# A recurrence with the backward heads' halves exchanged and the inverse transposed on TensorE, and two low-rank columns of the input projection made one

## The reference

```python
def rwkv_prep(u, shift_w, decay_b0, decay_up, iclr_b0, iclr_up, k_k, k_a, g_up):
    u = dwconv(u, shift_w).astype(jnp.float32)
    r, k, v, w_lo, a_lo, g_lo = jnp.split(u, [RWKV_W, 2 * RWKV_W, o1, o2, o3], axis=-1)
    kk = to_heads(k * k_k)
    kk = kk / jnp.maximum(jnp.sqrt(jnp.sum(kk * kk, axis=-1, keepdims=True)), 1e-12)
    for d in range(2):
        decay = jnp.exp(-DECAY_SCALE * jax.nn.sigmoid(decay_b0[d] + jnp.tanh(w_lo) @ decay_up[d]))
        a = jax.nn.sigmoid(iclr_b0[d] + a_lo @ iclr_up[d])
        k_d = k * (1.0 + (a - 1.0) * k_a)
...
def wkv_scan(r, k, v, decay, kk, a, s0, reverse, emit):
    def step(s, inp):
        r_t, k_t, v_t, w_t, kk_t, b_t = inp
        sa = -jnp.einsum("bhvk,bhk->bhv", s, kk_t)
        s = (s * w_t[:, :, None, :] + sa[..., None] * b_t[:, :, None, :]
             + v_t[..., None] * k_t[:, :, None, :])
        y = jnp.einsum("bhvk,bhk->bhv", s, r_t) if emit else None
        return s, y
```

## Time and profile before

| | us |
|---|---|
| median of 3 runs | 4267.63 |
| their range | 4267.39 to 4275.46 |
| the profiled execution | 4272.21 |
| its span | 4270.2 |
| PE busy in the span | 3939.6 |
| DVE busy | 2489.1 |
| ACT busy | 1605.8 |

### The profile page before, as it was taken

One profiled execution on the slowest core, in us unless ns is written; L12 is line 12 of the kernel. 1 busy time (PEld: TensorE's weight loads), 2 busy tenths in 40 slices (PEclk: granted clock), 3 DMA queues, 4 the chain that ended last, 5 costly groups with the idle time before them and its releaser, 6 DMA issues.

```text
span 4270.2 us, 85377 instructions
## 1 busy us (share of the span) xinstructions
PE 3939.6 (92%) x37243; PEld 3037.8 (71%) x37243; DVE 2489.1 (58%) x3146; ACT 1605.8 (38%) x1948; POOL 103.8 (2%) x96
## 2 busy tenths in 40 slices
PE   7987988999999897898999979888899999999996
PEld 5866885588887676887488668544677777777774
DVE  5966774322231675775443334563677777777774
ACT  3244332200021345333100242552566565656563
POOL 0000000000000000000000000000000000000000
PEclk9989999999999998999999989998899999999998
DMA  5430001121112441001222221402899999999995
GB/s 222 169 126 3 4 4 62 42 69 60 60 67 78 162 167 60 5 4 43 79 90 98 92 105 50 148 1 75 304 346 345 352 348 349 341 347 350 353 349 176
DMA packets 114120, 651.82 MB, mean 153 GB/s; under 512 B 15008, under 2 KB 15008, under 8 KB 55968
## 3 DMA queue, kind: packets, MB, share of 16 engines
q1 hardware_dynamic: 101344, 610.74, 38.3%
q0 software_dynamic: 12464, 36.38, 3.1%
HBM read 637.55 MB, written 27.46 MB: 156 GB/s over the span
## 4 chain that ended last, share of the span: by engine, by line
PE 83%; DVE 9%; ACT 4%; issue 2%; DMA 2%; SPq 0%; DVEq 0%; POOL 0%; POOLq 0%; ACTq 0%
PE psum L852 54%; PE psum L1603 16%; PE psum L1629 5%; PE psum L1620 4%; PE psum L1596 1%; DVE work L2020 1%; DVE xt L1988 1%; DVE work L2343 1%; PE psum L1587 1%; PE psum L1577 1%; DMA ring<-w_in 1%; PE psum L1456 1%; ACT work L2775 0%; DMA ring<-stream 0%; ACT work L3020 0%
## 5 line engine op out<-in xcount | busy, mean ns | idle before, releaser
L852 PE MATMUL psum<-ht_parts,ahead_parts 128*128 128x512 f32 (+3 forms) x2064 | 699.6, 355 | 2.9 <-DVE ht_parts L1752 2.2
L852 PE MATMUL psum<-work 64*64 64x64 f32 (+2 forms) x12950 | 548.4, 238 | 78.2 <-ACT work L2775 26.4
L852 PEld LDWEIGHTS psum<-work 64*64 64x64 f32 (+1 forms) x12950 | 441.4, 138 | 150.3 <-issue 70.8
L852 PE MATMUL psum<-work_parts,ring_parts 128*128 128x512 f32 (+1 forms) x1504 | 540.9, 360 | 0.0
L852 PE MATMUL psum<-work_parts,ahead_parts 128*128 128x512 f32 (+1 forms) x1408 | 495.3, 363 | 17.7 <-ACT work_parts L2629 15.6
L852 PEld LDWEIGHTS psum<-ht_parts,ahead_parts 128*128 128x128 f32 (+2 forms) x2064 | 379.2, 186 | 68.7 <-DVE ht_parts L1752 3.7
L852 PEld LDWEIGHTS psum<-work_parts,ring_parts 128*128 128x128 f32 x1504 | 286.3, 190 | 46.7 <-issue 1.7
L852 PEld LDWEIGHTS psum<-work_parts,ahead_parts 128*128 128x128 f32 x1408 | 266.3, 190 | 63.3 <-issue 21.8
L1603 PE MATMUL psum<-work_parts 128*128 128x512 f32 x1024 | 273.7, 394 | 0.7 <-DVE ring_parts L2468 0.5
L2468 DVE TENSOR_TENSOR ring_parts<-ring,work_parts 128x2048 fp32r<-128x2048 f32 x97 | 221.9, 2288 | 75.9 <-ACT work_parts L3094 75.9
L852 PE MATMUL psum<-xt_parts,ahead_parts 128*128 128x512 f32 (+5 forms) x656 | 233.2, 356 | 17.7 <-ACT xt_parts L2629 12.0
(11 more groups left out here) (351 smaller groups left out, 6780.2 us busy)
## 6 DMA issues: line engine op xcount, KB each, us to landing
ring<-stream SPq DMA_DIRECT2D x192, 1024.0 KB, 5.0
ring<-w_in SPq DMA_DIRECT2D x192, 1024.0 KB, 6.7
ht<-w_in SPq DMA_DIRECT2D x64, 1024.0 KB, 5.9
ht<-w_out SPq DMA_DIRECT2D x64, 1024.0 KB, 7.4
ring<-w_out SPq DMA_DIRECT2D x64, 1024.0 KB, 7.0
xt<-x_wide SPq DMA_DIRECT2D x8, 391.5 KB, 15.2
xt<-x_wide POOLq DMA_DIRECT2D x1, 3132.0 KB, 10.9
xt_rows<-xt POOLq DMA_DIRECT2D x8, 391.5 KB, 2.7
```

The costliest lines, as they stand in the source:

```text
L852: mm = pe.matmul(*args, **kwargs)
```

## The change

In the recurrence the tiles of direction 1 are held with their halves exchanged where that lets a group use all four quarters (`quarters`, with `way` "into", "from" or "same"). X is transposed on PE by a product with the unit matrix (`turned`, semaphore t) into banks 2 and 3 at every level, and DVE copies it (`turned` in vector, L2034 of the changed kernel); the product z and its write into Z remain for the last level alone. X is double-buffered. ACT writes the ones into X and copies the lower half of m1 (`ones`, `lower_part`). The products rhs and y are split into a part that doesn't need the newest operand and one that does. The order of the calls is new, and the decays are split over levels 3 and 4 of even chunks. In the input projection the columns 16 and 17 become one of 128 rows, `key_sum` steps follow one product sooner, and DVE copies the second low rank to its own tile.

```diff
-def in_half(n):
-
-    return n % 2 if n < 16 else (0, 0, 1, 0)[n - 16] if n < 20 else n % 2
+def in_half(u):
+
+    return u % 2 if u < 19 else (u + 1) % 2
...
-        for h in range(((2,) * 8 + (3, 1) + (2,) * 2)[slot]):
+        for h in range(1 if slot == 9 else 2):
             yield "product", n, h
-            if n >= 16:
-                yield "key", (n - 16) // 2, n % 2
+            if n >= 15:
+                yield "key", (n - 15) // 2, (n - 15) % 2
...
-                    a, b = ((0, 64), (64, 128), (0, 128), (0, 32))[n - 16] if 16 <= n < 20 else (0, 128)
+                    rows, terms = 32 if n == 18 else P, []
...
+                def halves_of(way, g, r):
+                    return {"same": (hs[r], hs[r]), "into": (hs[r], hs[r ^ g]), "from": (hs[r ^ g], hs[r])}[way]
...
+                def quarters(name, bank, off, terms, way, cols=64, step=64, swap=0, opens=True, first=False, last=True):
...
+                                    a, b = halves_of(way, g, r)
+                                    mm = matmul(psum[b, bank + (g ^ swap), off + step * p:off + step * p + cols], lhs(g, p, a), rhs(g, p, a),
...
+                def turned(i, n):
...
+                    quarters("t", 2, 0, [(op(R_x[i % 2]), unit_matrix)], "from", swap=1)
...
-                def level_xz(i, n):
+                def level_x(i, n):
                     kept("w", NL * (c0 + i) + n + 1)
...
-                        crossed_product("x", 0, 256, [(op(R_z[i % 2]), op(R_w))], False)
-                    heads_product("z", 2, [(op(R_w), op(R_z[i % 2]))])
+                    kept("t", NL * (c0 + i) + n + 1)
+                    quarters("x", 0, 256, [(op_z(i), op(R_w))], "into")
+
+                def last_z(i):
...
+                    quarters("z", 2, 0, [(op(R_w), op_z(i))], "same", swap=1)
...
+                def turned(i, n):
+                    ps = result("t", NL * (c0 + i) + n + 1, 2)
+                    dve.tensor_copy(R_z[i % 2], ps).then_inc(read_of["t"], 1)
...
-                    level(i, 0)
+                    level_x(i, 0)
+                    masked_m2(i)
                     if i == 0:
                         scale_conv(layer)
                     if more:
-                        sums_of_decays(i + 1)
+                        keys(i + 1)
+                    level_x(i, 1)
+                    if more:
+                        scaled_keys(i + 1)
+                    level_x(i, 2)
                     if i:
                         add_output(i - 1)
-                    level(i, 1)
                     if more:
-                        keys(i + 1)
+                        factors(i + 1)
+                    level_x(i, 3)
+                    if more:
+                        start_x(i + 1)
                     if i:
                         new_state(i - 1)
-                    level(i, 2)
                     if more:
-                        factors(i + 1)
-                        masked("q1", i + 1, 4, R_m1)
-                        start_z(i + 1)
-                    level(i, 3)
-                    if more:
-                        start_x(i + 1)
-                        masked("q2", i + 1, 6, R_m2)
-                    level(i, 4)
+                        masked_m1(i + 1)
+                    last_z(i)
+                    if i + 2 < NCHUNK:
+                        sums_of_decays(i + 2)
```

More of the change, by code:

```diff
@@ L1071, in q3 @@
+                    kept("q1", emitted(layer, i + 1))
+                    n, kr = keys_and_rows(i)
+                    quarters("q2", 6, 0, [(op(R_kh[i % 2]), kr)], "into", cols=n, step=128)
                 def q3(i):
[L1072 to L1080 removed]
@@ L1102, in level_w, with keys_turned @@
+                def keys_turned(i):
+                    quarters("kt", 2, 256, [(op(R_kh[i % 2]), unit_matrix)], "into")
                 def level_w(i, n):
@@ L1130, in solve, with rhs_values @@
+                def last_z(i):
+                    kept("w", NL * (c0 + i) + NL)
+                    kept("t", NL * (c0 + i) + NL)
+                    quarters("z", 2, 0, [(op(R_w), op_z(i))], "same", swap=1)
+                def rhs_values(i):
                     if i % 2 == 0 and i + 2 < NCHUNK:
                         kept("rate", c0 + i + 4)
-                    crossed_product("u", 3, 0, [(op(R_z[i % 2]), op(R_w1))], False)
-                def emit(i):
+                    kept("vb", c0 + i + 1)
+                    kept("q2", c0 + i + 1)
+                    quarters("part", 4, 0, [(part(R_m2[i % 2], 0), op(R_vt[i % 2]))], "from", opens=False, first=True, last=False)
@@ new lines, in rhs_state, with solve, emit_state @@
+                def rhs_state(i):
+                    pe.wait_ge(for_pe["part"], c0 + i + 1 + emitted(layer, i))
+                    pe.wait_ge(r_state, (NCHUNK - 1) * layer + i)
+                    quarters("rhs", 4, 0, [(keys_of(i), op(R_s))], "same", opens=False)
+                def solve(i):
+                    kept("z", c0 + i + 1)
+                    kept("rhs", c0 + i + 1)
+                    quarters("u", 4, 0, [(op_z(i), op(R_w1))], "into")
+                def emit_state(i):
+                    if emits(layer, i):
+                        if i + 1 < NCHUNK:
+                            kept("q2", c0 + i + 2)
+                        quarters("part", 6, 0, [(op(R_s), rows_of(i))], "same", opens=False, first=True, last=False)
@@ L1803, in token_shift @@
                 dve.wait_ge(raw_used, w.next(raw_used))
[L1804 to L1806 removed]
+                if n + 10 < 23:
+                    in_low(layer, n + 10)
             gate_read = {}
```

381 lines of the change are left out of this document (185 added, 196 removed).

## The result

The changed kernel is slower: 4323.7 us median (4319.4 to 4325.34, four runs) against 4271.55 (4267.39 to 4276.51, four runs), a ratio of 1.0123 with a 95% interval of 1.0111 to 1.0135. The forecast was 4276 with a range up to 4296: the sign of the sum was right, its size was not, and the time lies outside the range.

The account below looks back on a forecast made before the run. The prediction took PE in the recurrence to be paced by instruction arrival, 3.83 us per 128 loads. Its terms, -9.9 + 18 + 1 - 2.4 + 2 = +8.7 us on the 4267.63 median, gave 4276 us, range 4246 to 4296.

Parts of the forecast that it names:

- packets come closer together than 3.8 us: Recurrence: sign that the forecast is wrong, if instruction packets arrive faster once PE asks for them sooner.
- The rival of PE's own work: Recurrence: stops come from two-quarter products, not the fetch; PE gains 5.6 us a chunk, about 4165 us; chance 0.07.
- the fourth case below: Recurrence: case to believe if 128 KB of instructions were fetched ahead, so that stops at each packet needed another cause.
- The input projection: Merged columns 16 and 17 save 3.7 us in layer 0 and 6.2 in layer 1, together -9.9 us.
- The rival of the full 16.8 us: Input projection: merged columns give all 16.8 us if the scaled keys are ready sooner; 7 us down, no separate chance.
- The hand-over at the chunk's end: Recurrence: chain through PE, VectorE and ACT between chunks, 1.5 us longer than the instruction fetch that would hide it.
- Together 15.9 us: Recurrence: walked time from x of level 3 to x of the next chunk's level 1, against 14.4 us of packets.
- third rival: Recurrence: hand-over waits and instruction stops add up; a third of 6.6 us lost, 30.4 a chunk, about 4299; chance 0.08.
- -6.3: Recurrence: VectorE time a chunk saved by dropped Z updates, copies of ones, Z starts and half a mask pair, in us.
- +18 +1: Recurrence: +1.0 us in each of 18 output-emitting chunks, and +1 us in all for four second-layer chunks emitting nothing.
- -2.4 for the tail: After each layer's last chunk: the output's last two groups are shorter, -1.2 us a layer, -2.4 us.
- +2 for the first chunks: Each layer's first chunk: the convolution's scaling stands behind more VectorE work, +1 us a layer, +2 us.

Follow-up runs that it names:

- the copy moved: Changed kernel with VectorE's copy of the level-4 transposed X moved ahead of the state's second step and the mask; 1.0040 of the kernel before.
- x twice: Kernel before the change with the product x issued twice in levels 0 to 3, 128 more loads a chunk; 1.0160 of the kernel before.
- g outermost: Kernel of the copy moved, with the direction loop outermost in nine groups a chunk, so that they use two quarters at a time; 1.0059, 4287.6 us.
- the sums at level 1: Kernel of the copy moved, plus the state's addition before level 3's update, decays' sums behind level 1 and scaled keys behind level 2; 1.0007, 4267.27 us.

## Why the prediction was wrong

**Right.** The bound: PE is paced by its instructions. Among stops that follow each other after 126 to 129 loads, the distance is 3.3 us at the least and 3.6 to 3.9 in the mean of the first layer's window, in the kernel before, the changed one and four of the experiments (the copy moved, x twice, g outermost, the sums at level 1), and 96 added loads cost 2.9 us each chunk where PE needs 1.4. The sign "packets come closer together than 3.8 us" thus came true in part, 3.3 at the least, without making a chunk shorter. That PE's gain (5.6 us a chunk forecast, 4.5 measured) would buy nothing followed from the bound and held: busy time fell from 213 to 163 us in 236, and "issue" took it up. The rival of PE's own work is out. (It is the case that the sentence on the 128 KB means by "the fourth case below", to go by its condition.)

**Right, in part by luck.** The input projection: -9.9 forecast, -9.3 between the profiles, 7.7 by the ratio of the merged columns alone, with the new wait for the squares where it was put. In layer 0 two departures nearly cancel: the sum starts 0.7 us earlier than forecast, and its products take 1.45 us longer at the fallen clock, some of which comes back later. The rival of the full 16.8 us is out.

**Right in kind.** The hand-over at the chunk's end as the place of the loss, and its members in their order. One line moved in it brings back 35 us.

**Wrong in size.** The step that failed is "Together 15.9 us", the walk from x of level 3 to x of level 1, and the +1.0 a chunk made from it. Measured at its marks it is 12.3 + 5.2 = 17.5 us in the first layer and 12.6 + 5.4 = 18.0 in the second. Nearly all of the miss is in the part from level 3 to level 0, 10.95 forecast and 12.3 to 12.6 measured; the rest of a chunk was sized well (13.1 us for 13.4 to 13.9). The walk gave PE's products their own time, and set the packets' time beside it, 15.9 against 14.4, as if the longer of the two would hold. But a stop can fall between two products of the chain, as at 523.42, and then VectorE's and ACT's steps come after it and PE's next stop after them: the two add in part. The ends of the first layer's chunks give the shares of the 1.35 us. The end without such a stop lasts 11.4: 0.4 are steps that the walk had too short, such as z with its result (1.33 for 1.1). The other 0.9 are stops within the chain, but for some 0.1 that goes with the clock. The prediction had this as its third rival, at 0.08, with "a third of 6.6" for the share, 30.4 us a chunk, and about 4299 us. Measured are 30.7 and 31.9. That rival should have been the forecast: stops lie 3.3 to 4 us apart, and a chain of 16 us seldom avoids them all. Two more sizes were off. The walk's chunk was set against 28.5 us in both layers, though the second had 27.7; and VectorE's "-6.3" adds up to -6.8 by its own terms, which decided nothing.

**Not in the sum.** The clock. The prediction has no term for it and so kept, without a reason, the clock of the kernel before, 1.00 in the steady chunks. In the second layer's window PE is busy for 122 of 172 us, where it was 155, and the granted clock is 0.93 in the mean: 2.4 GHz for most of it and 1.2 for some. Where it falls, its price can be read at two places. Behind the wait for the copy, in which PE did nothing for 2.3 us, z ran at 1.2 GHz in two ends of the first layer and three of the second; these are its rows at 1.2 and at 2.4 GHz, and Z's update comes 2.15 us after the copy for 1.33:

```profile
649.75 1.86 PE L848 MATMUL psum<-work 64*64 64x64 f32 x30 [2.32 <-DVE work L2034]
...
435.82 1.09 PE L848 MATMUL psum<-work 64*64 64x64 f32 x30 [0.34 <-DVE work L2034]
```

And once in the second layer it fell onto the products of the decays, where level 2 to 3 took 11.1 us, for 9.2 two chunks before at the full clock:

```profile
1949.28 3.31 PE L848 MATMUL psum<-work,ring 65*128 65x128 f32 x16
1952.52 1.99 PE L848 MATMUL psum<-work 64*64 64x64 f32 x64
...
1885.15 2.05 PE L848 MATMUL psum<-work,ring 65*128 65x128 f32 x16
1887.13 1.46 PE L848 MATMUL psum<-work 64*64 64x64 f32 x64
```

That is 0.8 us five times and 1.9 once, 1.6 in the first layer and some 4 in the second. The second layer's six steady chunks take 6.7 us more than the first's, 188.5 for 181.8, so these places don't account for all of that, and the rest is open. In the kernel with g outermost a full clock showed no gain.

**The account** of 47.2 us between the profiles: -9.3 by the columns, +21.5 and +27.2 in the recurrences, of which some 6 can be put down to the clock, and 8 elsewhere, of which 3.1 behind the first recurrence and 3.3 in the second model, where no code changed. The forecast had +18 +1 for the chunks and +8.7 in all. The small terms, -2.4 for the tail and +2 for the first chunks, are of the size of what can't be told apart here.

**Open.** The reordered kernel without the stall at the chunk's end is still 11 us behind the merged columns alone. The change's 16 more loads a chunk are an eighth of a packet, 0.46 us by the pace and 11 us in 24 chunks, which would be all of it; no run took these loads away, so this is an estimate from the measured pace.

## What to carry to other kernels

When a stream of small instructions is paced by their arrival, count instructions first: here making products faster gained nothing, and 96 loads more cost 70 us. A hand-over through three engines isn't hidden by such a pace, since a stop can fall inside the chain and add to it (ends of 12.4 to 13.3 us for 11.4 without); in the order of a helping engine, the copy that the next product waits for goes ahead of work that is merely due. Moving a block out of a chain pays only if it lands where its engine idles: the same 2.5 us of sums gained nothing at level 0 and 13 us at level 1.

## What the runs showed of the hardware

The packets of instructions are 16 KB, 128 pairs of weight load and matmul on PE. When PE has used up what it has, the next 128 come 3.3 us later at the least and 3.7 in the mean, and that changed little with what PE did meanwhile: 3.67 in the changed kernel, 3.88 in the kernel before, 3.65 with two-quarter products off the chain, each in the window from 416 to 652 us. The Trainium skill, "Advanced Engine Details and Errata", section ISA Cache, gives "Only 2 cache lines!" of 16 KB; the size agrees, and no run here counts the lines. The 128 KB that it gives for TensorE, by division eight packets, would let PE run through many more than 128 pairs after each wait, and these stops don't show that. Sixteen 64x64 products with their 32 loads take 0.47 us of issue on four quarters. Behind waits of 2.32 and 4.33 us in which PE did nothing, the granted clock was at 1.2 GHz: thirty matmuls of z took 1.86 us there and 1.09 at 2.4 GHz, and the key sum's four, most of them at 1.2, took 2.90 us for 1.45.
